# Splitting weight tiles on GpSimd in quarter-tile operations, in a decoder layer on one core

## The reference, cut to what matters

```python
h = rmsnorm(x, norm_w) * (1 + scale) + shift          # scale, shift, gate from c @ w_ada
proj = h @ w_in                                       # 1024 x 9736 weights, the result split in 13 parts
att = sliding_window_attention(rope(aq), rope(ak), av, sinks)   # 16 heads, 4 kv heads, window 128
y_att = (att * silu(az)) @ w_att_branch
hm = mlstm_chunkwise(silu(conv(mq)), silu(conv(mk)), mv, i_pre, logf)   # 4 heads of 256
y_m = (norm(hm) * sigmoid(mo) * silu(mz)) @ w_m_branch
out = rmsnorm(x + gate * ((sigmoid(ga) * y_att + sigmoid(gm) * y_m) @ w_out), final_norm_w)
```

## Time and profile before

| what | value |
|---|---|
| median of 3 runs | 1438.28 us (1438.25 to 1438.99) |
| span of the profiled execution | 1435.3 us |
| mean granted TensorE clock | 0.979 |
| TensorE busy | 1340.0 us, 93% |
| VectorE busy | 750.4 us, 52% |
| ScalarE busy | 396.6 us, 28% |
| GpSimd busy | 491.6 us, 34% |

### The profile page before, as it was taken

How to read it: one execution, slowest core, us unless ns; L and a number is a source line. 1 busy time by engine, 2 the same in 40 slices (tenths; PEclk the granted TensorE clock), 3 DMA queues, 4 the chain that set the end, 5 groups by cost and what they waited for, 6 DMA issues and landing times.

```text
span 1435.3 us, 19403 instructions
## 1 busy us (share of the span) xinstructions
PE 1340.0 (93%) x6846; PEld 1138.8 (79%) x6846; DVE 750.4 (52%) x1297; ACT 396.6 (28%) x926; POOL 491.6 (34%) x248
## 2 busy tenths in 40 slices
PE   2399998999989999999999999999999999899998
PEld 2297796978867888877988898889789888788886
DVE  5979888695776000065256426633672421366445
ACT  5342634334342010013221322233223311311111
POOL 4613204132045343273054205412531333335230
PEclk9599999999999999999999999999999999999999
DMA  9501102011021121050041004101310123322502
GB/s 350 137 15 30 45 2 59 15 29 29 0 58 35 54 88 59 15 162 16 1 117 44 0 0 132 29 0 41 91 44 15 44 74 98 107 76 68 193 16 103
DMA packets 119830, 89.28 MB, mean 62 GB/s; under 512 B 13305, under 2 KB 111721, under 8 KB 118894
## 3 DMA queue, kind: packets, MB, share of 16 engines
q1 hardware_dynamic: 116288, 76.16, 17.8%
q10 hardware_dynamic: 3502, 12.61, 2.5%
HBM read 80.35 MB, written 8.41 MB: 62 GB/s over the span
## 4 chain that ended last, share of the span: by engine, by line
PE 78%; DVE 14%; issue 4%; ACT 2%; DMA 1%; POOL 1%; DVEq 0%; ACTq 0%; SPq 0%; POOLq 0%
PE pp L527 22%; PE pp L529 22%; PE pp L528 22%; DVE conv L1382 2%; PE pp L713 2%; PE pp L723 2%; PE pp L633 1%; DVE prob L1232 1%; DVE y_lo L1289 1%; PE pp L624 1%; PE pp L602 1%; PE pp L616 1%; PE pp L705 1%; PE pp L617 1%; PE pp L718 1%
## 5 line engine op out<-in xcount | busy, mean ns | idle before, releaser
L482 POOL TENSOR_TENSOR w_hi<-raw,ones 128x1024 fp32r<-128x1024 f32 x101 | 201.4, 1994 | 828.6 <-ACTq L346 492.0
L527 PE MATMUL pp<-h_hi,w_hi 128*128 128x512 f32 x912 | 363.1, 398 | 14.8 <-DVE h_lo L1115 9.5
L528 PE MATMUL pp<-h_lo,w_hi 128*128 128x512 f32 x912 | 357.6, 392 | 0.0
L529 PE MATMUL pp<-h_hi,w_lo 128*128 128x512 f32 x912 | 357.1, 392 | 0.0
L484 POOL TENSOR_TENSOR w_lo<-raw,w_hi 128x1024 fp32r<-128x1024 f32 x101 | 257.2, 2546 | 7.9
L527 PEld LDWEIGHTS pp<-h_hi,w_hi 128*128 128x128 f32 x912 | 172.9, 190 | 52.6 <-issue 10.3
L529 PEld LDWEIGHTS pp<-h_hi,w_lo 128*128 128x128 f32 x912 | 172.6, 189 | 36.7
L528 PEld LDWEIGHTS pp<-h_lo,w_hi 128*128 128x128 f32 x912 | 172.9, 190 | 35.2
L527 PE MATMUL pp<-w_hi,h_hi 128*128 128x384 f32 (+1 forms) x512 | 162.1, 317 | 0.6 <-DVE roped L1209 0.6
L529 PE MATMUL pp<-w_hi,h_lo 128*128 128x384 f32 (+1 forms) x512 | 158.2, 309 | 0.0
L528 PE MATMUL pp<-w_lo,h_hi 128*128 128x384 f32 (+1 forms) x512 | 158.0, 309 | 0.0
(11 more groups left out here) (216 smaller groups left out, 1947.6 us busy)
## 6 DMA issues: line engine op xcount, KB each, us to landing
raw<-w_in SPq DMA_DIRECT2D x72, 512.0 KB, 3.8
w_mod<-w_ada SPq DMA_DIRECT2D x7, 1024.0 KB, 11.1
x_in<-x SPq DMA_DIRECT2D x4, 1024.0 KB, 8.2
raw<-w_att SPq DMA_DIRECT2D x8, 512.0 KB, 5.1
merged_dram<-mix_a ACTq DMA_DIRECT2D x8, 512.0 KB, 2.6
w_gate<-w_ada ACTq DMA_DIRECT2D x8, 512.0 KB, 3.5
raw<-w_m SPq DMA_DIRECT2D x8, 512.0 KB, 3.7
mix_in<-merged_dram ACTq DMA_DIRECT2D x8, 512.0 KB, 3.3
```

The lines of the kernel that those rows point to most:

```text
L482: pool.tensor_tensor(hi, raw[:, s, :, :], one, ALU.mult).then_inc(slot_hi[s], 1)
L527: pe.matmul(o, lh, rh, start=first, stop=False)
L528: pe.matmul(o, lh, rl, start=False, stop=False)
L529: return pe.matmul(o, ll, rh, start=False, stop=last)
```

## The change

Inside `split`, each of the two GpSimd operations over 1024 columns becomes four over 256 columns, two blocks of 128 each. The semaphore that each raised is raised by the fourth. The wait between high and low stays where it was, after the fourth high operation. Waits on load and release, the order of the splits, `y_hi`, `dec` and all other engines' instructions are as before. GpSimd thus issues 808 operations for the 101 splits in place of 202.

```diff
                 pool.wait_ge(slot_loaded[s], 16 * loads)
-                pool.tensor_tensor(hi, raw[:, s, :, :], one, ALU.mult).then_inc(slot_hi[s], 1)
+                parts = [slice(q * KT // 4, (q + 1) * KT // 4) for q in range(4)]
+                for q in parts:
+                    ins = pool.tensor_tensor(hi[:, q, :], raw[:, s, q, :], one[:, q, :], ALU.mult)
+                ins.then_inc(slot_hi[s], 1)
                 after(pool, slot_hi[s], uses + 1)
-                pool.tensor_tensor(lo, raw[:, s, :, :], hi.bitcast(F32), ALU.subtract).then_inc(slot_split[s], 1)
+                for q in parts:
+                    ins = pool.tensor_tensor(lo[:, q, :], raw[:, s, q, :], hi[:, q, :].bitcast(F32), ALU.subtract)
+                ins.then_inc(slot_split[s], 1)
```

## The result

| | before | changed |
|---|---|---|
| median | 1438.26 us | 1391.63 us (1391.58 to 1391.74, 4 runs) |
| span of the profiled execution | 1435.3 us | 1389.9 us |
| mean granted TensorE clock | 0.979 | 0.992 |

The ratio is 0.968, with an interval of 0.967 to 0.970: 46.6 us faster, two and a half times the 18.5 us forecast and outside the range (1404 to 1438). The direction was right, the size was not.

What follows compares the result with a forecast made beforehand. VectorE, stalled by whole GpSimd operations at a shared SBUF port, was taken to make TensorE wait. Gains of 13 + 2 + 1 + 1 + 1.5 = 18.5 us gave 1438.3 - 18.5 = 1419.8 us, range 1404 to 1438.

Steps and rivals of the forecast that it cites:

- What bounds the kernel: Whole kernel: TensorE waits for VectorE, which whole GpSimd operations hold up at a shared SBUF port, taken in turns.
- The hold of a quarter operation, 0.48 and 0.59 us: Splits: 256 columns hold VectorE 0.48 (high) and 0.59 us (low); a split's hold becomes 4.3 in place of 3.6.
- Stage A, 13 us of 23: Attention heads: loss of 5.8 us per head falls to 2.6, gain 13 in all, ends 23 and -8.
- lateness adds up to the next block's `prob`: Stage A: 4.2 us of lateness less 2.2 absorbed; TensorE loses 2.0 per head plus 0.6 for half a clock fall.
- `mk_t` "four dependent steps meet 2.1 in place of one low operation's 2.0, 0": The 6.3 us wait for `mk_t`: four steps lose 4 x 0.53 = 2.1 in place of 2.0, gain 0.
- The first convolution's new wait of 1.8 us: First stage C slot behind the mask: split ends at 629.5, TensorE newly waits 1.8 us; net gain there 1.
- The clock, counted in stage A alone (5 us): Stage A: a granted-clock fall, 0.63 over 3.4 us, costs 1.3 us more, taken for each of four heads.
- Start, +8.1 and -6: Path to first product saves 8.1; `x_mod` and `h_lo` tiles lose 6.9, about 1 absorbed; net gain 2, ends -4 and +8.
- The last split, 1.8 us left of 4.6: Last four splits: 4.6 us before use, four times 0.7 is 2.8; 1.8 remains and nothing is lost.
- the port does come free between parts without a semaphore: Rival on splits claimed the opposite: GpSimd runs four parts as one block, stalls stay, 1440 us; chance 0.10.
- a quarter operation doesn't hold VectorE for as long as a half one: Rival claimed the opposite: a quarter holds 0.84 us, a split 6.7 in place of 3.6, 1460 us; chance 0.10.
- lateness is only spread: Rival for stage A and start: VectorE's losses equal GpSimd's whole hold however cut, gains cancel, 1437 us; chance 0.12.

Runs made afterwards that it cites:

- the floor run: Changed kernel with work left out: after the first five splits, up to the first output half, each makes only 4 of 128 columns; 1376.3 us, ratio 0.959.
- 23.9 alone: Against the kernel before, quarter pieces only in the splits during the four attention heads, whole operations elsewhere; 1413.5 us, ratio 0.983.
- `rest_only`: Against the kernel before, quarter pieces only in the splits after the attention heads, whole operations before; 1419.5 us, ratio 0.988.
- the four widths: Split operations in pieces of 1024 (kernel before), 512, 256 (changed kernel) and 128 columns everywhere; 1438.26, 1421.6, 1391.63 and 1394.9 us.

## Why the prediction was wrong, step by step

The cause was right and the sizes were not, in all three parts: by the table above the start gave 6.6 us where 2 was forecast, stage A 23.2 where 13 was, and the rest 15.7 where 3.5 was. What failed:

- *What bounds the kernel*: right. VectorE's stalls behind whole GpSimd operations, taken in turns, were the cause; the floor run puts their cost at 60 us or more.
- *The hold of a quarter operation, 0.48 and 0.59 us, from "a fixed 0.11 us per operation"*: this step failed. Measured for a dependent step: 0.23 and 0.36. The error was in the point at 512 columns, 0.84, where a dependent step waits 0.66: it came from `y_hi` in turns with `y_lo`, a queued pair with other operations, while the one at 1024 came from dependent steps. Two kinds of operations on one line gave the fixed part the wrong sign; it is about -0.2 us, not +0.11. So a split's hold fell from 3.5 to 2.4 us where 4.3 was forecast.
- *Stage A, 13 us of 23*: the largest single term and the most mis-sized one; it gave 23.2 in the trace and 23.9 alone. The first half (the waits for `prob` and the keys vanish since 2.2 us is absorbed) is what happened. The second half, that lateness adds up to the next block's `prob` and TensorE loses 2.0 + 0.6 per head, was too dear: 1.8 us of waits for `prob` remain in four heads and no clock fall, and against the floor run the heads lose 1.6 us each. And the whole loss, 5.8 per head, was too small: it is 29.5/4 = 7.4. Part of that is the clock. The earlier trace rows was read as 0.63 over 3.4 us, but its window begins 0.9 us before the fall, which is at 0.50 for all of its 3.4 us and costs 1.7, not 1.3.
- *`mk_t` "four dependent steps meet 2.1 in place of one low operation's 2.0, 0"*: failed by the same hold. Four steps now lose about 4 x 0.3 in place of 2.0 or more, and the 6.3 us are gone.
- *The first convolution's new wait of 1.8 us*: the split ran from 589.3 to 597.8 in the changed kernel, 8.5 us where 9.1 was forecast, and TensorE's matmul of that slot followed without a gap. The two `xpad` waits went. GpSimd's timeline there:

```profile
589.32 2.78 POOL L484 TENSOR_TENSOR w_hi<-raw,ones 128x256 fp32r<-128x256 f32 x4
592.18 5.65 POOL L488 TENSOR_TENSOR w_lo<-raw,w_hi 128x256 fp32r<-128x256 f32 x4
```

- *The clock, counted in stage A alone (5 us)*: the falls after `y_lo` and `xpad` were put at nothing, without a reason. They cost up to 1.7, 1.7 and 3.4 us more, and in the first trace of the changed kernel they went too. `rest_only` gained 17.9 where the prediction's terms sum to 3.5. In its trace the waits for `xpad` and `mk_t` (9.3) are gone, those for both `y_lo` and `num` are 4.2 less, and of these falls only one, of 3.4 us, is left in D2, which gives back about 5 us: 18 to 19 in all.
- *Start, +8.1 and -6*: 9.8 gained on the path to the first product, then 3.2 given back. `h_lo` loses 0.34 to 0.54 us per tile against 1.22, 3.7 in eight, and `x_mod` another 1.9 in five; of these 5.6 TensorE, which works behind them, absorbed 2.4 and not 1:

```profile
L1120 DVE TENSOR_TENSOR h_lo<-x_mod,h_hi x8: 1560/1692/1756, 53.3 to 69.0; 128x1024 fp32r<-128x1024 f32 x8
```

- *The last split, 1.8 us left of 4.6*: its end in the changed kernel is 1332.00 + 2.81 = 1334.8, the use at 1335.20. 0.4 left, no loss; but a split costs 1.0 us more there, (4.6 - 0.4)/4, not 0.7. The 0.7 was the growth of what a split holds VectorE, used as the growth of GpSimd's own time. These are two quantities: the first fell, the second grew by more. GpSimd's busy time went up by 171 us, not by some 60:

```profile
1332.00 2.81 POOL L488 TENSOR_TENSOR w_lo<-raw,w_hi 128x256 fp32r<-128x256 f32 x4
```

```profile
1335.20 0.39 PE L532 MATMUL pp<-w_hi,g_hi 128*128 128x512 f32 x1
```

- *Rivals*: the port does come free between parts without a semaphore, and a quarter operation doesn't hold VectorE for as long as a half one. Of "lateness is only spread" a part is true: the floor run shows up to 15 us still lost.
- *GpSimd's own time*: doubling a piece's duration and taking off that of the next wider one gives a fixed part of 2 x 0.615 - 1.041 = 0.19 and 2 x 0.399 - 0.615 = 0.18 us per operation. By the Trainium skill (GPSIMD Engine Reference, section 3.1) I had estimated a fixed 0.2 us on each instruction, and the traces agree. It was right on GpSimd, and would have been wrong on this kernel, in which TensorE waits for no quarter split.

The range failed because every unknown was sized by the same hold and the same belief in accumulated lateness; its low end left 1391 out although the bounds "all of it goes" stood in the text (23 for stage A, 8 for the start, and 18.7 of waits listed for the rest).

## What to carry to other kernels

A long operation of one engine that shares a port is paid for by the other engine's short ones: compare the slowest with the median of the same VectorE line, and if the gap is about one GpSimd operation, cut that operation. How far is set by place: finer where the other engine is dense and the result is needed late, coarser where the result is needed soon, since every further piece costs GpSimd some 0.17 us or more (1.0 us for six in the last splits). When many waits share one cause, price the case that all of them go, falls of the clock included, and give it a real chance.

## What the runs showed of the hardware beyond that

A VectorE instruction that needs the port waits for the duration of the GpSimd instruction in progress less 0.38 us, from 128 to 1024 columns and for both operations here, so that at 128 columns a dependent one is hardly held at all (0.02 and 0.08 us). The Trainium skill (SBUF — State Buffer, section "SBUF: two separate sides") says that the shared ports are an exclusive lock that is held for the full instruction and not a split of bandwidth. The traces agree with the lock, and they show that the two engines' recorded times overlap wherever the port changes hands. Take a convolution step that was held up and count back its own time, 1.284 us, from its recorded end: that point lies 0.20 us before the recorded end of the GpSimd piece it waited for (0.20 to 0.21 in all 124 steps of the four widths that were held for more than 0.05 us). The same done with a GpSimd piece that waited for such a step gives a point 0.14 us before the step's recorded end (0.13 to 0.17 in 98 cases). With the 0.04 us from one step to the next these make the 0.38. From the kernel before, a convolution step and the GpSimd operations before and behind it:

```profile
622.84 3.30 DVE L1382 SCALAR_TENSOR_TENSOR conv<-xpad,taps_q,conv 128x1024 f32<-128x1024 f32 x1
622.33 2.73 POOL L484 TENSOR_TENSOR w_lo<-raw,w_hi 128x1024 fp32r<-128x1024 f32 x1
625.03 2.87 POOL L482 TENSOR_TENSOR w_hi<-raw,ones 128x1024 fp32r<-128x1024 f32 x1
```

The step ends at 622.84 + 3.30 = 626.14, so its own 1.284 begin at 624.86, and the low operation ends at 625.06, 0.20 later. The high operation ends at 627.90, so its own 1.89 begin at 626.01, 0.13 to 0.14 before the step's end.

Which VectorE instructions are held shows in their longest times before. Those that read PSUM (`pp`) are not: `rot_s` took 469 to 482 ns in all 32, `prob_t` 669 to 692 in all 60, though 4 and 9 of them ran wholly beside a split operation. The prediction's count of eleven such operations in a block left these out rightly.

```profile
L1240 DVE TENSOR_TENSOR prob_t<-pp,turned_new x32: 669/680/682, 106.3 to 429.6; 128x512 f32<-128x512 f32 x32
L1240 DVE TENSOR_TENSOR prob_t<-pp,turned_old x28: 670/680/692, 113.2 to 429.0; 128x512 f32<-128x512 f32 x28
```

Each fall of the clock to 1.2 GHz before, 3.4 or 6.8 us long, stood behind a wait of TensorE of 1.3 us or more or a row of them close together. In the changed kernel a single wait of 1.5 us for `prob_t` and three of 0.8 for `num` were followed by none. One of 2.2 for `y_lo` was followed by none in the first profile and by a fall of 3.4 us in the second, of the same kernel. Which waits bring a fall I can't tell from these runs.
